# A fused encoder block on one core: PSUM banks, wait places and queue order changed in five places

## What is computed

```python
h = rms_norm(x, pre_mix_norm)
proj = h @ w_in                                   # 1024 x about 3600
fq, fk, fv, ff, gq, gk, gv, gb, ga, gz = split(proj)
fox_o = rms_norm(forgetting_attention(fq, fk, fv, log_sigmoid(ff + bias)))   # 8 heads of 64, causal
cq, ck, cv = silu(causal_conv(gq, gk, gv))        # 4 heads of 128
gdn_o = rms_norm(gated_delta_chunked(cq, ck, cv, g, beta)) * silu(gz)
x = x + rms_norm(concat(fox_o, gdn_o) @ w_out, post_mix_norm)
h = rms_norm(x, pre_mlp_norm)
x = x + rms_norm(square(relu(h @ w_up)) @ w_down, post_mlp_norm)
```

## Time and profile before

| | |
|---|---|
| median of three runs | 1496.18 us (1494.28 to 1497.17) |
| the profiled execution: its own time, its span | 1496.14 us, 1494.4 us |
| PE busy | 1391.5 us, 93% of the span |
| DVE, ACT, POOL busy | 964.4 us (65%), 662.1 us (44%), 643.5 us (43%) |
| mean DMA traffic | 119 GB/s |
| chain that ended last, by engine | PE 76%, DVE 11%, issue 4%, POOL 4%, ACT 3% |

### The profile page before, as it was taken

One profiled execution on the slowest core, in us unless ns is written; L12 is line 12 of the kernel. 1 busy time (PEld: TensorE's weight loads), 2 busy tenths in 40 slices (PEclk: granted clock), 3 DMA queues, 4 the chain that ended last, 5 costly groups with the idle time before them and its releaser, 6 DMA issues.

```text
span 1494.4 us, 20689 instructions
## 1 busy us (share of the span) xinstructions
PE 1391.5 (93%) x7373; PEld 1175.5 (79%) x7373; DVE 964.4 (65%) x1498; ACT 662.1 (44%) x1406; POOL 643.5 (43%) x518
## 2 busy tenths in 40 slices
PE   6899999988989899798799979999999999999997
PEld 4688888877878889697678767888888788888885
DVE  6877777755566665765534697767766585444557
ACT  6554334435464564554524352333333244445453
POOL 3643322316364462652600365666666364443001
PEclk9999999999999999999899999999999999999999
DMA  6133333245032031011322234444444895333633
GB/s 206 43 114 113 114 113 113 95 154 165 25 101 71 29 100 44 15 43 45 96 87 85 71 106 155 152 138 144 143 150 150 310 338 194 99 96 95 211 99 141
DMA packets 135325, 177.88 MB, mean 119 GB/s; under 512 B 10492, under 2 KB 82732, under 8 KB 135224
## 3 DMA queue, kind: packets, MB, share of 16 engines
q1 hardware_dynamic: 135224, 176.56, 36.8%
HBM read 124.05 MB, written 52.48 MB: 118 GB/s over the span
## 4 chain that ended last, share of the span: by engine, by line
PE 76%; DVE 11%; issue 4%; POOL 4%; ACT 3%; DMA 1%; SPq 0%; DVEq 0%; POOLq 0%; ACTq 0%
PE ps L2662 6%; PE ps L2950 6%; PE ps L2952 6%; PE ps L2951 6%; PE ps L2937 6%; PE ps L2939 6%; PE ps L2614 6%; PE ps L2938 6%; PE ps L2616 6%; PE ps L2615 6%; PE ps L2789 3%; PE ps L2889 2%; PE ps L2891 2%; PE ps L2890 2%; PE ps L2667 2%
## 5 line engine op out<-in xcount | busy, mean ns | idle before, releaser
L2950 PE MATMUL ps<-db_hi,da_hi 128*128 128x512 f32 x448 | 175.3, 391 | 3.7 <-DVE db_lo L2226 3.6
L2951 PE MATMUL ps<-db_lo,da_hi 128*128 128x512 f32 x448 | 174.4, 389 | 0.0
L2952 PE MATMUL ps<-db_hi,da_lo 128*128 128x512 f32 x448 | 174.3, 389 | 0.0
L2224 DVE TENSOR_TENSOR da_lo<-a_raw,da_hi 128x512 fp32r<-128x512 f32 x112 | 85.3, 762 | 121.0 <-ACT da_hi L1701 121.0
L1701 ACT ACTIVATE da_hi<-a_raw 128x512 fp32r<-128x512 f32 x112 | 70.7, 631 | 159.4 <-PE ps L2952 138.9
L2937 PE MATMUL ps<-bt_hi,ring_hi 128*128 128x512 f32 x320 | 127.6, 399 | 6.3 <-DVE ring_lo L2146 5.2
L2939 PE MATMUL ps<-bt_hi,ring_lo 128*128 128x512 f32 x320 | 126.2, 394 | 0.0
L2938 PE MATMUL ps<-bt_lo,ring_hi 128*128 128x512 f32 x320 | 125.4, 392 | 0.0
L2614 PE MATMUL ps<-i_bt_hi,i_ring_hi 128*128 128x512 f32 x280 | 111.4, 398 | 3.2 <-DVE i_u L1890 3.2
L2616 PE MATMUL ps<-i_bt_hi,i_ring_lo 128*128 128x512 f32 x280 | 110.7, 396 | 0.0
L2615 PE MATMUL ps<-i_bt_lo,i_ring_hi 128*128 128x512 f32 x280 | 110.4, 394 | 0.0
(11 more groups left out here) (361 smaller groups left out, 3724.9 us busy)
## 6 DMA issues: line engine op xcount, KB each, us to landing
a_raw<-act_dram SPq DMA_DIRECT2D x112, 256.0 KB, 2.6
act_dram<-s_act SPq DMA_DIRECT2D x64, 256.0 KB, 2.0
wd<-in_w_down_dram SPq DMA_DIRECT2D x15, 1024.0 KB, 7.7
act_dram<-c SPq DMA_DIRECT2D x48, 256.0 KB, 4.9
w_top<-in_w_up_dram SPq DMA_DIRECT2D x18, 512.0 KB, 4.6
w_bot<-in_w_up_dram SPq DMA_DIRECT2D x16, 512.0 KB, 5.7
i_top<-in_w_in_dram SPq DMA_DIRECT2D x14, 512.0 KB, 4.0
i_bot<-in_w_in_dram SPq DMA_DIRECT2D x14, 512.0 KB, 5.3
```

The source lines that it names most:

```text
L2950: nc.tensor.matmul(acc, da_hi[s][:, cols], db_hi[s][:, :], start=start, stop=False, skip_group_check=True)
L2951: nc.tensor.matmul(acc, da_hi[s][:, cols], db_lo[s][:, :], start=False, stop=False, skip_group_check=True)
L2952: return nc.tensor.matmul(acc, da_lo[s][:, cols], db_hi[s][:, :], start=False, stop=stop, skip_group_check=True)
```

## The change

1. **The gate products' wait.** In `gate_products` the second group's wait is split: its first 12 matmuls start without one, the next 12 wait for part (5, 1) of `i_bt`, the last 12 for part (3, 1).
2. **ACT's and DVE's order after it.** ACT makes `bt_hi_part(4, 2)` and `i_hi(0, 5)` ahead of the two reads of the gate products. DVE makes `c_out(0, 6)` and `c_out(0, 7)` between `bt_lo_part(4, 2)`, `i_lo(0, 4)` and `i_lo(0, 3)`.
3. **The first queries.** `queries(0)` moves ahead of ACT's last copy of the projection, and on POOL ahead of the first two powers.
4. **The up projection's loads.** `load_pair(2)` goes ahead of the loop, and the loop loads pair f + 3 instead of f + 2 before the stores of pair f.
5. **Banks after the last fill.** All eight outputs o of the last head's scan go to bank 1 and have a semaphore of their own, `late_out`, set by the matmul that ends them. ACT reads them after that and no longer after `state_ready`; `scan_first` no longer waits for `o_read`, `scan_second` does. Attention chunks 83, 85 ... 95 are turned into bank 3, the even ones stay in bank 6, and a turn waits for the copy of the chunk two before it. Tiles 55, 57 ... 63 have their output in bank 2, the even ones in bank 7, with the wait for the read of the tile two before. The first user of each of the three banks waits until the last three fills are read (`fills_read`).

The core of the diff:

```diff
-        at("act", b - (4.0 if i else 0.64), "queries", i)
-        at("pool", b - 3.0 if i else b + 0.4, "queries", i)
+        at("act", b - (4.0 if i else 3.5), "queries", i)
+        at("pool", b - 3.0, "queries", i)
...
+LATE_SCANS = [item[1:] for item in _items[_free:] if item[0] == "scan_o"]
+LATE_TURNS = [FOX_CHUNK[item[1:]] for item in _items[_free:] if item[0] == "turn"]
+LATE_TILES = [item[1] for item in _items[_free:] if item[0] == "pv" and item[2] == 0]
+LATE_OUT = numbered(LATE_SCANS)
+def turn_bank(n):
+    return 3 if n in LATE_TURNS and n % 2 == 1 else 6
+def out_bank(i):
+    return 2 if i in LATE_TILES and i % 2 == 1 else 7
...
+            load_pair(2)
             for f in range(FP - 1):
-                if f + 2 < FP:
-                    load_pair(f + 2)
+                if f + 3 < FP:
+                    load_pair(f + 3)
...
             c11_out(1)
+            bt_hi_part(4, 2)
+            i_hi(0, 5)
             act.wait_ge(params_loaded, 16 * PARAM_LOADS)
...
-            i_hi(0, 5)
-            bt_hi_part(4, 2)
             i_hi(0, 4)
...
             def o_out(h, c):
-                act.wait_ge(state_ready, h * NCHUNK + c + 1)
+                if (h, c) in LATE_OUT:
+                    act.wait_ge(late_out, LATE_OUT[(h, c)])
+                    src = late_scan[:, 0:P]
+                else:
+                    act.wait_ge(state_ready, h * NCHUNK + c + 1)
+                    src = scan_ps[:, 2 * P:3 * P]
...
-                        take({1: 1, 3: 3, 6: 1}.get(n, 0))
+                        take({1: 1, 3: 4, 6: 1}.get(n, 0))
...
-            i_lo(0, 4)
-            i_lo(0, 3)
...
+            c_out(0, 6)
+            i_lo(0, 4)
+            c_out(0, 7)
+            i_lo(0, 3)
...
                 for n, (first_k, b_hi, b_lo) in enumerate(terms):
+                    if half == 1 and n >= 1:
+                        pe.wait_ge(x_bt_lo, I_BT[(5 if n == 1 else 3, 1)])
...
-            pe.wait_ge(x_bt_lo, I_BT[(3, 1)])
             gate_products(1, [left[0], (0, i_bt_hi[5][:, :, :], i_bt_lo[5][:, :, :]), (HK, i_bt_hi[3][:, :, :], i_bt_lo[3][:, :, :])])
...
+            def fills_read():
+                for name in FILLS[-NFILL_BANKS:]:
+                    wait_read(pe, name)
...
             def turn(i, c):
-                if n >= 1:
-                    wait_copied(n - 1)
+                if TURN_BEFORE[n] is not None:
+                    wait_copied(TURN_BEFORE[n])
+                if n == LATE_TURNS[0]:
+                    fills_read()
...
             def times_v(i, c):
-                    if i >= 1:
-                        pe.wait_ge(fox_read, i)
+                    if OUT_BEFORE[i] is not None:
+                        pe.wait_ge(fox_read, OUT_BEFORE[i] + 1)
...
             def scan_first(h, c):
-                pe.wait_ge(o_read, n)
+                if (h, c - 1) not in LATE_OUT:
+                    pe.wait_ge(o_read, n)
...
             def scan_second(h, c):
+                o = late_scan[:, 0:P] if late else scan_ps[:, 2 * P:3 * P]
+                if late and c == 0:
+                    fills_read()
+                elif late:
+                    pe.wait_ge(o_read, n)
+                if c > 0:
+                    nc.tensor.matmul(o, qdT[s][:, c, :], state[:, :], start=True, stop=False)
+                out = nc.tensor.matmul(o, a_t[s][:, c, :], values, start=(c == 0), stop=True)
+                if late:
+                    out.then_inc(late_out, 1)
```

32 lines of the change are left out of this document (21 added, 11 removed).

## The result

The changed kernel takes 1488.8 us (median of seven runs, 1486.86 to 1490.79), the kernel before 1496.98 in the runs beside it: ratio 0.9944, 95% interval 0.9932 to 0.9957. A second set gave 1488.2 us and 0.9934 (0.9921 to 0.9948). It is 8 to 9 us faster; 13.2 were forecast, and 1488.8 lies 0.8 us above the range. The profiled execution took 1488.51 us.

The account below looks back on a forecast made before the run. PE bounds the up projection; elsewhere its waits and low clock cost time. Gains of 7.1 (start), 0.6 (queries), 1.0 (loads) and 4.5 us (banks) sum to 13.2, from 1496.2 to 1483.0 us; range 1480 to 1488.

Parts of the forecast that it names:

- I take no fall, since the nearest row in length is the 1.93 us one: Input projection: clock stays up after product 6's new 1.8 us wait, gaining 7.1 us; with a fall, 5.6.
- What is late next is nothing that I find up to 77.8: Input projection: after product 4 no further late operand up to 77.8 us, so the 7.1 us gain stands.
- the chain behind decay feeds all that follows: Heads' start: POOL's decay about 0.6 us earlier passes on to everything behind it, a gain of 0.6 us.
- Up to 708.80 nothing changes: Heads' end: the new banks change nothing before 708.80 us, where PE's 2.83 us wait is for ACT's exponential.
- weights that come a pair earlier buy nothing there: Up projection: with PE busy 256.94 of 257.00 us, earlier loads gain nothing; only the 0.97 us wait near it can go.
- Rival (e): Up projection: SP's stores stand behind a waiting load and land late, PE waits each pair: 1500.9 us, chance 0.02.
- (a): The start's new wait lowers the clock and POOL blocks the norm at the end: 1485.5 us, chance 0.20.
- (b): Input projection: the stall only moves, product 4 waits again for u3: 1487.5 us, chance 0.10.

Follow-up runs that it names:

- start_only: The kernel before with only the split gate wait and the new ACT and DVE order: 1493.60 us, ratio 0.9976.
- changed_again: The changed kernel as it is, timed and traced a second time: 1488.2 us, ratio 0.9934 to the kernel before.
- bank_output_only: The kernel before with only the late scan outputs moved to bank 1, turns and attention outputs in their old banks: 1496.5 us, ratio 0.9994.
- six_first: The changed kernel with ACT and DVE finishing product 6's operands before they turn to `i_bt` 7: 1487.39 us, ratio 0.9930 to the kernel before.
- queries_only: The kernel before with only the first queries moved earlier on ACT and POOL: 1497.81 us, ratio 1.0005.
- six_first_gates_late: The changed kernel with product 6's operands first, product 5's sum earlier and four DVE gate operations one product later: 1490.72 us, ratio 0.9955 to the kernel before.
- banks_only: The kernel before with only the three more banks in the last phase: 1494.97 us, ratio 0.9986.
- bank_turns_only: The kernel before with only every other late turn in bank 3, scan and attention outputs as before: 1498.57 us, ratio 1.0006.
- loads_only: The kernel before with only the up projection's loads one pair earlier: 1495.66 us, ratio 0.9986.

## Why the prediction was wrong

- **Parts 1 and 2: 7.1 us forecast up to the instruction at 77.8, 5.3 in the trace there, 4.7 by 89 us.** The step that failed is "I take no fall, since the nearest row in length is the 1.93 us one": the clock fell behind product 6's wait in all three traces that have parts 1 and 2 in this order, 2.27 us long here, 2.16 in start_only and 1.80 in changed_again, which is the very length that was forecast. It costs 1.6 us. With the fall the prediction had 5.6, and changed_again has 5.6 at 77.8. Nor does a longer wait decide it: in bank_output_only 2.45 and 3.20 us had no fall behind them. The rest of the mechanism ran as forecast: no wait at the second gate group, none ahead of product 4. "What is late next is nothing that I find up to 77.8" holds in the changed kernel, but the look stopped there: 0.6 us go at DVE's sums by 89 us. It would not have held without the fall: in six_first product 3 waits 2.09 us, the lead is 7.0 us at 77.8 and 5.3 by 89, so a PE that comes earlier meets DVE's queue, which is busy 94 to 99% there; I had followed u3 and never added that queue up.
- **Part 3: 0.6 us forecast, 0.5 there and then covered.** POOL's decay came 0.6 us closer to ACT's last post-processing, as forecast (it starts 2.66 us behind it, 3.27 before). Counted from 89 us, the first product of the delta rule's preparation (340.08 before) is 0.5 us earlier in queries_only and 0.4 to 0.5 in six of the seven other traces that have the part (six_first_gates_late lost 5 us before), and at most 0.3 in those without it. Five us on it is -0.6 to 0.9 us, by where the clock is low. That "the chain behind decay feeds all that follows" is thus neither shown nor excluded by the total: queries_only is 1.0005 (0.9996 to 1.0014).
- **The heads' middle: nothing forecast, 1.5 us lost in the first pair of traces.** Changed_again takes 610.6 us there as well, though 354.4 in the shorter stretch and not 355.7. The eight kernels without part 3 take 607.0 to 613.6 us there, mean 609.7; those with it 608.6 to 610.7 (leaving out six_first_gates_late, which has a wait of its own there). A loss by part 3 is thus not shown and not excluded. What differs is the granted clock, 0.98 before and 0.97 now; the kernel before was traced 0.6 us under the mean, and a sum made against one execution inherits that.
- **Ahead of the last phase: nothing forecast, 0.7 us lost (0.3 in changed_again).** "Up to 708.80 nothing changes" failed: the new banks serve the turns from 698.33 on. The longer wait for DVE's copy, 1.88 us for 0.91, comes with a clock of 0.82 over the stretch (0.84 in banks_only), where it is 0.99 before and 0.97 or more in every trace with two or three of the banks as before, bank_turns_only included.
- **Part 4: 1.0 us forecast at its upper bound, 1.9 in the traces.** The wait at 917.83 went, and PE's other lost time with it. In the runs of loads_only it is 0.9986 (0.9976 to 0.9996), about 2 us. The assumption that "weights that come a pair earlier buy nothing there" was read from 256.94 of 257.00 us in one trace; other traces of the same order lose up to 2.3 us more. Rival (e), the stores, did not happen.
- **Part 5: 4.5 us forecast, 3.6 in the changed kernel (4.4 in banks_only), less what was lost ahead of it; about 2 us in the runs of banks_only (0.9986, 0.9974 to 0.9999).** The mechanism ran as forecast: the norm at 736.42 just ahead of POOL at 736.67, 0.35 us long; the products with v in one piece of 2.00 us; 737.14 against the first turn at 706.87 is 30.27 us, where 738.0 and 708.80 make 29.2: about 1 us is lost on the way, where the clock of the first stretch shown above is 0.68, against 0.84 for the same instructions before (708.80 to 723.72). By the rule on the shared port of the Trainium skill (SBUF — State Buffer, "SBUF: two separate sides") whoever starts first decides; the traces agree where the order is clear, with 0.35 us for a norm that starts 0.25 us ahead of POOL; of 2.51 us before and 2.50 in bank_turns_only they cannot say who was first, as norm and POOL start within 0.02 us of each other. As to its rule on banks used in turn (TensorE: Matmul & The Clock Gate, "A second HAM failure mode: psum-queue depth-cycling"), the clock from the first of the new turns to the product with w_out is 0.83 before, 0.82 in the changed kernel and 0.86 in banks_only: no run here shows that cost over the phase, only a low clock that comes earlier in it.

Sum: the misses are 2.4 (start), 0.6 (queries), 1.5 (heads' middle), 0.7 (ahead of the last phase), 0.9 (banks) and 0.5 ahead of 40 us, 6.6 in all, less 1.1 won in the up projection and behind it: 5.5 us, from 13.2 to 7.7. In the runs' medians the gain is 8.2. So no one step explains the miss: the largest that is shown is the clock's fall behind product 6 (1.6 us), the heads' 1.5 us go with a lower clock and are there again in changed_again, and why the runs of the changed kernel have the lower clock stays open. The likeliest rival, (a), had the clock's fall right and the norm wrong; (b) did not come, as product 4 has no wait; what moved, moved beyond the stretch that I had looked at. The range's low end took 2.0 us for the queries where their own paragraph has 2.5; with 2.5 it would be 1479.7, which changes nothing here.

## What to carry to other kernels

When a stall goes near the front of a pipeline, follow every engine's queue until the other engines have slack again, not only until the wait in question is gone: in six_first a third of what was won at product 4 was lost again within 20 us, at DVE's sums. Two cures for waits that follow each other do not add up: the split wait alone gives 0.9980 and the new order alone 0.9964, but both together 0.9976. Do not read from the length of a wait whether the clock falls behind it; carry both cases in the sum. Where an untouched stretch of 610 us differs by up to 6.6 us between traces, cost terms of 1 us need a stretch that repeats (the up projection did, within 0.2 us), and many runs.
